# Adding the attention mask of the neighbouring tiles in PSUM on VectorE, in place of two bf16 products on TensorE

## The reference

```
def sink_attend(qb, keys, values, masks, sinks):
    ...
    for kk, m in zip(keys, masks):
        s = jnp.einsum('bqhgd,bkhd->bhgqk', qb, kk).astype(jnp.float32) * scale
        if m is not None:
            s = jnp.where(m, s, -jnp.inf)
        parts.append(s)
    ...
    p = jax.nn.softmax(jnp.concatenate(parts + [sink], axis=-1), axis=-1).astype(qb.dtype)
    ...
def windowed_attention(q, k, v, k_ctx, v_ctx, sinks):
    ...
        kpos = q0 + offs
        mask = (jnp.abs(qi[:, None] - offs[None, :]) <= WINDOW) & ((kpos >= 0) & (kpos < L))[None, :]
        return sink_attend(qb, (kb, k_ctx), (vb, v_ctx), (mask, None), sinks)
```

## Time and profile before

| | |
|---|---|
| Median of three runs | 2724.66 us |
| The profiled execution | 2726.17 us, span 2723.6 us |
| Mean granted clock of TensorE | 0.985 |
| Busy in the span: TensorE | 2614.6 us (96%) |
| VectorE | 2012.8 us (74%) |
| ScalarE | 1359.3 us (50%) |
| GpSimd | 613.1 us (23%) |
| Attention | 253 to 520 us of the span |
| Mask products (L923) | 128 |

### The profile page before, as it was taken

The page is one execution under the profiler, slowest core; times in us unless marked ns, Lnnn a source line. Parts: engine busy times, 40 slices in busy tenths (PEclk is TensorE's granted clock), DMA queues, the critical chain, the costliest instruction groups (busy, mean ns, idle before and its releaser), DMA issues. The chain is left out here.

```text
span 2723.6 us, 44405 instructions
## 1 busy us (share of the span) xinstructions
PE 2614.6 (96%) x14920; PEld 1176.8 (43%) x14923; DVE 2012.8 (74%) x5303; ACT 1359.3 (50%) x3150; POOL 613.1 (23%) x467
## 2 busy tenths in 40 slices
PE   7999999999899999999999889998999999999996
PEld 2444666544433333333444365444333343333342
DVE  4996666585588887788888465855898888888875
ACT  1112666343256666666666251431666666666651
POOL 0000000111023233233322221100233323233322
PEclk9999999999999999999999999999999999999998
DMA  9776500200399999999999732016999999999996
GB/s 366 266 266 200 187 17 17 76 39 39 146 371 368 332 337 353 327 337 377 352 334 339 248 146 84 39 47 241 362 366 340 343 318 341 335 372 332 338 345 205
DMA packets 151614, 697.65 MB, mean 256 GB/s; under 512 B 25505, under 2 KB 30881, under 8 KB 99162
## 3 DMA queue, kind: packets, MB, share of 16 engines
q1 hardware_dynamic: 103964, 555.09, 52.3%
q0 software_dynamic: 46832, 136.58, 20.3%
q10 hardware_dynamic: 592, 3.16, 0.3%
HBM read 597.50 MB, written 129.13 MB: 267 GB/s over the span
## 5 line engine op out<-in xcount | busy, mean ns | idle before, releaser
L1842 ACT ACTIVATE xT<-xt_blocks 32x256 f32<-32x256 f32 x2176 | 900.4, 414 | 39.0 <-DVE xt_blocks L1663 11.6
L1920 PE MATMUL exG<-ring,xT 128*32 128x512 f32 (+2 forms) x2608 | 572.1, 593 | 1.3 <-DMA ring<-in_exp_w_up_dram 0.7
L1678 DVE STREAM_TRANSPOSE ex_hT<-ex_h 32x64 f32<-32x64 f32 x2240 | 528.7, 236 | 33.6
L1920 PE MATMUL exG<-wide_w,xT 128*32 128x512 f32 (+2 forms) x1472 | 385.2, 600 | 0.7 <-DVE xT L1657 0.7
L1589 POOL DMA_INDIRECT y_scratch<-wide_w,idx_out x203 | 335.8, 1654 | 149.0 <-issue 66.6
L1920 PE MATMUL exG<-wide_t,xT 128*32 128x512 f32 (+2 forms) x960 | 361.5, 603 | 7.8 <-issue 4.4
L1576 POOL DMA_INDIRECT wide_t<-u_scratch,idx x144 | 152.6, 1060 | 937.8 <-DVE idx_out L1714 742.5
L1920 PEld LDWEIGHTS exG<-ring,xT 128*32 128x32 f32 (+2 forms) x2608 | 199.5, 129 | 314.7 <-issue 312.2
L1854 ACT ACTIVATE ex_e<-exG 128x256 f32<-128x256 f32 x142 | 54.4, 383 | 503.7 <-PE exG L1920 500.2
L1955 PE MATMUL exD<-ring,ex_hT 128*32 128x512 f32 (+2 forms) x1304 | 296.2, 597 | 2.5 <-DVE wide_w L1706 2.5
L1668 DVE TENSOR_TENSOR ex_h<-ex_e,exG 128x256 f32<-128x256 f32 x142 | 86.7, 611 | 190.9 <-ACT ex_e L1854 162.3
(11 more groups left out here) (369 smaller groups left out, 3275.8 us busy)
## 6 DMA issues: line engine op xcount, KB each, us to landing
ring<-in_exp_w_gate_dram SPq DMA_DIRECT2D x64, 1024.0 KB
ring<-in_exp_w_up_dram SPq DMA_DIRECT2D x64, 1024.0 KB
ring<-in_exp_w_down_dram SPq DMA_DIRECT2D x64, 1024.0 KB
wide_t<-in_exp_w_gate_dram SPq DMA_DIRECT2D x34, 1024.0 KB
wide_t<-in_exp_w_up_dram SPq DMA_DIRECT2D x34, 1024.0 KB
wide_t<-in_exp_w_down_dram SPq DMA_DIRECT2D x34, 1024.0 KB
wide_w<-in_exp_w_gate_dram SPq DMA_DIRECT2D x32, 1024.0 KB
wide_w<-in_exp_w_up_dram SPq DMA_DIRECT2D x32, 1024.0 KB
```

Of the source, the lines that this page charges most:

```text
L1678: last = dve.transpose(hT[m * UNIT:(m + 1) * UNIT, par].rearrange("p (k t) -> p k t", k=FK)[:, :, a * UNIT:(a + 1) * UNIT], hid[a * UNIT:( ...
L1842: last = act.activation(xT[m * UNIT:(m + 1) * UNIT, par, :, a * UNIT:(a + 1) * UNIT], parts[a * UNIT:(a + 1) * UNIT, m], ACT.Copy)
L1920: last = pe.matmul(psG[par][p:p + m], xT[:, par, k, p:p + m], ring[s % RING][:, 0:2, k * FF:(k + 1) * FF], start=k == 0, stop=k == KT - 1)
```

## The change

The two mask products go, and so do the bf16 identity, its conversion and TensorE's wait for the set-up. A new function `cover(p)` on VectorE waits for the scores of pair p and adds the mask in place in PSUM, for both heads in one `tensor_tensor`: 128 partitions x 2 heads x 2 neighbouring tiles x 128 keys in an inner tile, one neighbouring tile in an edge tile. The bf16 mask is the second operand, the same for both heads. The first reduction of the pair now waits for a new semaphore `masked`, which the addition raises. The near score products become the last of the pair, and their signal is VectorE's.

```diff
--- before.py
+++ after.py
@@ -703,7 +703,6 @@
             with ExitStack() as ctx:
                 sb, ps, sem = pools(ctx)
                 qT = first_q[:].rearrange("p (i k c) -> p i k c", i=2, k=KT)
-                identb = sb("identb", [P, P], BF16)
                 nsink = sb("nsink", [P, H])
                 mx, nm = sb("mx", [P, 2, 2]), sb("nm", [P, H])
                 rs, es, den = sb("row_sum", [P, H]), sb("sink_exp", [P, H // 2]), sb("den", [P, H // 2])
@@ -718,6 +717,7 @@
                 q_in = [sem(f"q_in{i}") for i in range(2)]
                 w_in, zeroed, zero_out = sem("w_o_in"), sem("zero_rows_done"), sem("zero_rows_out")
                 far_mm, score_mm, max_done, exp_done = sem("far_mm"), sem("score_mm"), sem("max_done"), sem("exp_done")
+                masked = sem("masked")
                 T_first, T_rest, copied_a, copied_d, pv_mm, o_done = (sem(n) for n in (
                     "probT_first", "probT_rest", "probT_a", "probT_d", "pv_mm", "o_done"))
                 sink_in, sink_done, den_own, den_done, spread_done, den_mm, share_done = (sem(n) for n in (
@@ -784,13 +784,21 @@
 
                     @block.vector
                     def _(dve):
-                        dve.tensor_copy(identb[:], ident[:]).then_inc(set_up, 1)
                         dve.tensor_scalar(nsink[:], sink[:], -1.0, None, ALU.mult).then_inc(set_up, 1)
-                        dve.wait_ge(set_up, 2)
+                        dve.wait_ge(set_up, 1)
+
+                        def cover(p):
+                            t = p // PAIRS
+                            tiles, (W, S) = near_tiles(t), width(p)
+                            edge = [i for i, k in enumerate(tiles) if k != t]
+                            dve.wait_ge(score_mm, p + 1)
+                            both = pair[p % 2][:, 0:2 * S].rearrange("p (j s c) -> p j s c", j=2, c=P)[:, :, edge[0]:edge[-1] + 1:2]
+                            gone = mask[:, tiles[edge[0]] - t + 1:tiles[edge[-1]] - t + 2:2]
+                            dve.tensor_tensor(both, both, gone.unsqueeze(1).to_broadcast([P, 2, len(edge), P]), ALU.add).then_inc(masked, 1)
 
                         def largest(p, j):
 
-                            dve.wait_ge(score_mm, p + 1)
+                            dve.wait_ge(masked, p + 1)
                             at_least(dve, max_done, p - 1)
                             dve.tensor_reduce(mx[:, p % 2, j:j + 1], halves_of(p, pair[p % 2])[j], AX, ALU.max).then_inc(own, 1)
 
@@ -832,11 +840,13 @@
                             dve.wait_ge(pv_mm, 4 * n + 4)
                             dve.tensor_tensor(oT[:, 4 * c:4 * c + 4, t * P:(t + 1) * P], psO[:], share[:], ALU.mult).then_inc(o_done, 1)
 
+                        cover(0)
                         largest(0, 0)
                         largest(0, 1)
                         shift(0)
                         for p in range(N + 2):
                             if p + 1 < N:
+                                cover(p + 1)
                                 largest(p + 1, 0)
                             if p < N:
                                 copy(p)
@@ -891,8 +901,6 @@
 
                     @block.tensor
                     def _(pe):
-                        pe.wait_ge(set_up, 1)
-
                         def scores(p):
                             t, h = heads(p)
                             kv, k = h // 4, h // 2
@@ -909,18 +917,14 @@
                                     last = pe.matmul(sc[j][:, W:S], q[j], far[j], start=True, stop=True)
                                 last.then_inc(far_mm, 1)
                                 for j in range(2):
-                                    pe.matmul(sc[j][:, 0:W], q[j], near[j], start=True, stop=False)
+                                    last = pe.matmul(sc[j][:, 0:W], q[j], near[j], start=True, stop=True)
                             else:
                                 pe.matmul(sc[0][:, W + P:S], q[0], far[0][:, P:CTX], start=True, stop=True).then_inc(far_mm, 1)
                                 pe.matmul(sc[1][:, W:S], q[1], far[1], start=True, stop=True)
                                 pe.matmul(sc[0][:, W:W + P], q[0], far[0][:, 0:P], start=True, stop=True)
                                 pe.wait_ge(far_mm, p + 1)
                                 for j in (1, 0):
-                                    pe.matmul(sc[j][:, 0:W], q[j], near[j], start=True, stop=False)
-                            edge = [i for i, k in enumerate(tiles) if k != t]
-                            for j in range(2):
-                                over = sc[j][:, 0:W].rearrange("p (s c) -> p s c", c=P)[:, edge[0]:edge[-1] + 1:2]
-                                last = pe.matmul(over, identb[:], mask[:, tiles[edge[0]] - t + 1:tiles[edge[-1]] - t + 2:2], start=False, stop=True)
+                                    last = pe.matmul(sc[j][:, 0:W], q[j], near[j], start=True, stop=True)
                             last.then_inc(score_mm, 1)
 
                         def turn(p):
```

## The result

The changed kernel took 2740.75 us (median of four runs, 2734.51 to 2747.64) against 2724.7 before (four runs): a ratio of 1.0057, interval 1.0034 to 1.0081. Five more runs, against 17 of the kernel before, gave 2738.41 against 2726.71 (medians), ratio 1.0048, interval 1.0035 to 1.0061. It is slower, by 9 to 22 us in the first comparison and 9.5 to 17 in the second; 2736 was forecast. The profiled execution took 2734.51 us, its span is 2732.1.

A forecast was written before the change was run, and what follows sets the result against it. Attention was taken as bound by a chain through VectorE, ScalarE and TensorE that closes over two head pairs. Inner tiles +9.8, edge tiles +1.9 and start -0.6 gave +11.1 us on 2724.7, so 2736 us, stated range 2728 to 2747.

The forecast's parts named there:

- a chain over three engines that closes over two pairs: Inner tiles: VectorE, ScalarE, TensorE, VectorE form a loop without slack, 8.60 us, the next 8.17; 24 such loops.
- Price of the addition: VectorE's mask addition of 512 elements in an inner tile: 0.69 us taken from L833, bounds 0.37 and 1.08.
- the dear: Rival: PSUM addition costs as the strided row does, +22 us, 2747; chance 0.11.
- the cheap rival: Rival: addition near the 748 ns row's rate, or no link price; +2.4 to +5 us, 2727 to 2730; chance 0.13.
- The link: On VectorE the first reduction waits for the addition's end; 0.04 us charged per loop.
- Products out: Without the two bf16 mask products VectorE's signal comes 0.32 us earlier per inner-tile loop.
- Inner tiles +9.8: Six inner query tiles: 0.73 us in, 0.32 out, +0.41 per loop, times 24 loops gives +9.8 us.
- Edge tiles +1.9: First and last query tiles: 0.45 us in, 0.21 out, +0.24 per loop, times 8 loops gives +1.9 us.
- Start -0.6: Start of attention: TensorE no longer waits for the bf16 identity, -0.6 us.
- TensorE stands 0.75 us per two pairs: Sign in the profile: TensorE idle before transposes, released by ScalarE's exponential, 0.75 us per two pairs in place of 0.10.
- TensorE's queue as the bound: Rival: TensorE sets the pace, so removing its products makes the kernel faster, 2715 us; chance 0.06.
- The clock: Rival: TensorE's waits drop its granted clock of 1.00 to 1.2 GHz in places; 2780 us or so; chance 0.02.

The follow-up runs named there:

- no_mask: The changed kernel without the addition, so no mask is applied at all: inner tiles 193.40 us, attention 259.92 us; whole time not comparable.
- apart_wait_first: Kernel before, with edge-tile nm computed per head and TensorE's identity wait only before the first mask product; ScalarE's nm wait stays first: attention 263.23 us, ratio 0.999.
- nm_wait_last: Kernel before with one edit, ScalarE's wait for nm placed behind its two other waits: inner tiles 202.82 us, attention 268.90 us, ratio 1.0008.

## Why the prediction was right

- *The bound is a chain over three engines that closes over two pairs.* Shown: the odd pairs' additions cost 0.1 us in all, the even pairs' the whole 9.9, and a handoff later by 0.08 us costs 24 times that.
- *Price of the addition, 0.69 (0.37 to 1.08).* 0.700 for 512 elements, 0.432 for 256 (0.41 was used). Against L833 (691 ns) the write to PSUM, the gap and the bf16 operand together add 0.01 us, so the dear and the cheap rival fall.
- *The link, 0.04.* Measured 0.04. The Trainium skill ("VectorE: DVE Perf Modes", "The DRAIN you can't avoid") measures no extra cost for a semaphore between two VectorE copies. Here the addition pushes the reduction by 0.74; an unlinked one, started 0.08 before the addition's end as the copy is, would be pushed by 0.62, an estimate, since no run has it. That makes 0.12 per loop, and the +7.0 that the rule gave for the inner tiles was too little against +9.93. The forecast told that section too narrowly: the section also says that an instruction which is not held starts earlier, and the copy here does start earlier. What these rows speak against is only that the semaphore costs nothing.
- *Products out, 0.32.* no_mask gives 0.31 per loop (200.83 - 193.40 = 7.43, by 24).
- *Inner tiles +9.8.* 210.76 - 200.83 = +9.93.
- *Edge tiles +1.9.* Two pairs of the last tile took 7.73 (reductions at 510.67 and 518.40) in place of 7.48 (500.13 and 507.61): +0.25, forecast +0.24. All in all the edge tiles took 2.2 us more (+1.66 in the first and +0.69 in the last, less 0.11 behind the last pair). How near that comes to +1.9 is in part luck: the last tile gives under the 0.96 that four loops ask for, and the first tile changes by 2.3 us between two profiles of one program.
- *Start -0.6.* TensorE's first product began 0.05 us after the stage did (252.39 against 252.34), in place of 0.66 (253.78 against 253.12): -0.61. The first reduction, which has the addition ahead of it, came 2.64 us after the stage began, in place of 3.18; in the second profile 1.76, because the clock fell later.
- *TensorE stands 0.75 us per two pairs.* Its loads do: 0.94 - 0.55 + 0.36. Its busy time lacks less, 13.34 us of 201 or about 0.6 in each of 22.9 loops, because it counts products, which run on for a while behind their loads: 0.33 us is missing ahead of the transposes (392.63 + 0.91 = 393.54, then 393.87), and the rest inside them.
- *What stood off.* The whole time, 2738 to 2741, lies a few us above 2736. The second comparison, +11.7 between the medians, lies near the forecast of +11.1, though attention had grown by 13.0 in its profile and the rest of that execution was 5.9 shorter, so that it lies so near is partly chance. The first comparison's +16 is above it, with an interval of +9 to +22. The inner tiles, which agree to 0.01 between two profiles, carry the proof, not the whole time.
- *Rivals.* TensorE's queue as the bound: its products are gone, it stands for ScalarE in every loop, and the kernel became slower. The clock: 1.00 in the inner tiles.

## What to carry to other kernels

Where three engines pass one tile round, follow the loop through the timeline from one start to the next of the same kind. If it closes without a gap, every step of it costs in full, however idle its engine is, and a step in the sister loop costs nothing as long as it fits into that loop's slack (the 0.41 us of the odd pairs did); trying the edit on every second round finds out which. Judge such an edit by the stretch that it touches, since gains and losses of 2 us cancel in the whole time.

## What the hardware showed that was not expected

**The order of met waits.** A pair's exponentials have two semaphores to wait for, three where p is a multiple of 4, and `nm` is the one that comes last. Where the program waited for it first, 34 first exponentials of the inner tiles started 0.03 to 0.04 us after `nm` in the kernel before and 35 in apart_wait_first (the other 12 in each 0.34 us or more after it); where it waited for it last, none started under 0.09, and 32 in nm_wait_last took 0.09 to 0.12. The changed kernel, with its wait in the first place too, has 24 at 0.03 to 0.04 and 11 at 0.06 to 0.07, which was not followed up.

**The clock at the start of attention varies.** TensorE has no product for 2.2 to 2.8 us between the stages, and within 1.5 us of the start of attention its clock falls to 1.2 GHz, in every kernel here. When it falls and for how long differs between executions of the same program. From 256 to 268 us, the changed kernel's two profiles (the granted clock is the number after the five busy times):

```profile
256.00:268.00 12.00, 9.34 (x58) 6.22 (x58) 8.04 (x18) 6.38 (x17) 0.00 (x0) 0.86 1.04 205
```

```profile
256.00:268.00 12.00, 9.07 (x38) 5.89 (x36) 6.62 (x14) 5.54 (x14) 0.00 (x0) 0.50 1.02 207
268.00:272.00 4.00, 4.00 (x29) 2.73 (x27) 2.44 (x6) 2.02 (x6) 0.00 (x0) 0.84 1.04 201
```

In the second the granted clock is 0.50 all through, and 0.84 in the 4 us after that; the first tile took 2.3 us more. Ahead of that it had started at full clock, so its first reduction came 0.9 us sooner. The first profile has two slow stretches with 2.4 GHz between them (one row of the second profile, then two of the first):

```profile
254.24:255.24 1.00, 0.95 (x9) 0.98 (x11) 0.51 (x1) 0.00 (x0) 0.53 (x1) 1.00 0.00 0
```

```profile
256.40:259.20 2.80, 1.31 (x8) 0.84 (x8) 2.27 (x5) 1.95 (x5) 0.00 (x0) 1.00 1.03 197
259.40:262.40 3.00, 3.00 (x13) 2.18 (x14) 1.01 (x3) 1.45 (x4) 0.00 (x0) 0.50 1.04 203
```

In the first of these two TensorE was busy for 1.31 of 2.80 us, and then the clock fell again. For comparison the kernel before, at 0.82:

```profile
256.00:268.00 12.00, 10.48 (x68) 6.90 (x66) 7.89 (x16) 6.22 (x16) 0.00 (x0) 0.82 1.04 213
```

Over all ten profiles the time at 1.2 GHz is about 3, 7 or 14 us (the table's last column). In the changed kernel attention was 1.4 us longer with 7 us more of it. What decides it was not tried.
